# Norming the first chunk's mixer outputs in two steps, with the convolution's heads last

## What is computed

```python
def _mixer_block(h, w_in, ..., g_head_out, w_out):
    proj = h @ w_in                                   # 11 pieces of 256 columns
    out_a = _sgu_mixer(su, sv, w_sgu, b_sgu, g_sgu_v)
    out_b = _dilated_mixer(qd, kd, heads(dv)).reshape(B, S, MIX_W)
    out_c = _short_conv_mixer(cb, cc, cx, conv_w)
    out_d = _stick_breaking(qs, ks, heads(bv)).reshape(B, S, MIX_W)
    cat = jnp.concatenate([out_a, out_b, out_c, out_d], axis=-1).reshape(B, S, N_MIX_HEADS, HEAD_DIM)
    cat = _rms(cat, g_head_out.reshape(N_MIX_HEADS, HEAD_DIM)).reshape(B, S, D_MODEL)
    return cat @ w_out

def chunk(xc):                                        # retrieval, 128 tokens
    q = (xc @ w_q).reshape(C, PEER_HEADS, 2, PEER_HALF)
    ...                                               # top 16 pairs of keys per head: eidx, g
    a = jnp.einsum('thkd,td->thk', u_tab[eidx], xc)
    w = g * jax.nn.gelu(a)
    return jnp.einsum('thk,thkd->td', w, v_tab[eidx])
```

## Time and profile before

| what | value |
|---|---|
| time, median of 3 runs | 2979.73 us (2978.29 to 2980.22) |
| the profiled execution | 2974.2 us |
| its span, first to last instruction | 2972.4 us |
| TensorE busy | 2661.7 us (90%) |
| VectorE busy | 2007.6 us (68%) |
| ScalarE busy | 1501.0 us (50%) |
| moved by DMA | 1198.56 MB, mean 403 GB/s |

### The profile page before, as it was taken

One profiled execution on the slowest core, in us unless ns is written; L12 is line 12 of the kernel. 1 busy time (PEld: TensorE's weight loads), 2 busy tenths in 40 slices (PEclk: granted clock), 3 DMA queues, 4 the chain that ended last, 5 costly groups with the idle time before them and its releaser, 6 DMA issues.

```text
span 2972.4 us, 29543 instructions
## 1 busy us (share of the span) xinstructions
PE 2661.7 (90%) x8492; PEld 1468.9 (49%) x8492; DVE 2007.6 (68%) x5227; ACT 1501.0 (50%) x4099; POOL 1159.0 (39%) x1028
## 2 busy tenths in 40 slices
PE   8998989999999879998899988999989988777777
PEld 7753555754565335654455544654456533222222
DVE  3478678767689964556557987577668897454444
ACT  3246546468355543448434564458825554333333
POOL 0233433235434434344433444334434344343332
PEclk9999999999999989999999999999999999999999
DMA  5699999889999999999999999999999999999998
GB/s 231 245 398 421 415 421 421 359 358 407 421 421 421 421 411 419 421 421 408 421 421 405 421 421 421 420 406 421 421 421 411 380 422 421 422 421 422 422 421 347
DMA packets 167343, 1198.56 MB, mean 403 GB/s; under 512 B 19856, under 2 KB 20112, under 8 KB 22160
## 3 DMA queue, kind: packets, MB, share of 16 engines
q0 software_dynamic: 147456, 1073.81, 87.2%
q1 hardware_dynamic: 19728, 122.87, 10.2%
HBM read 1194.50 MB, written 2.10 MB: 403 GB/s over the span
## 4 chain that ended last, share of the span: by engine, by line
DMA 32%; PE 31%; DVE 7%; ACT 7%; issue 2%; POOL 0%; SPq 0%; POOLq 0%; ACTq 0%; DVEq 0%
DMA ring<-in_uv,idx 31%; PE psY L1271 21%; PE psP L1151 4%; DVE ring L1550 3%; PE psP L1144 3%; ACT L915 1%; ACT L1106 1%; ACT ring L1115 1%; ACT wgt L1111 1%; ACT gl L1106 1%; DMA wr<-in_w_out 0%; PE psO L1237 0%; POOL ring L892 0%; PE psT L1129 0%; DVE fm L1520 0%
## 5 line engine op out<-in xcount | busy, mean ns | idle before, releaser
L1271 PE MATMUL psY<-ring 128*128 128x512 f32 x3916 | 1840.7, 613 | 256.3 <-ACT ring L1115 251.7
L892 POOL DMA_INDIRECT ring<-in_uv,idx x1024 | 1158.8, 1132 | 1785.2 <-PE psY L1271 1545.5
L1550 DVE CUSTOM_DVE_ANT_0 ring<-ring,htok 128x1024 f32<-128x1024 f32 x1024 | 1239.4, 1222 | 673.0 <-DMA ring<-in_uv,idx 667.1
L1271 PEld LDWEIGHTS psY<-ring 128*128 128x128 f32 x3916 | 726.1, 194 | 1219.0 <-issue 1211.4
L1106 ACT ACTIVATE gl<-adot 128x1 f32<-128x1 f32 x1024 | 204.8, 200 | 1006.8 <-DVE adot L1550 1003.6
L1115 ACT ACTIVATE ring<-cst,wgt 128x128 f32<-128x128 f32 x979 | 393.2, 402 | 31.9
L1111 ACT ACTIVATE wgt<-gate,gl 128x1 f32<-128x1 f32 x1024 | 301.7, 295 | 33.2
L1144 PE MATMUL psP<-hT,wr 128*128 128x256 f32 (+1 forms) x1632 | 306.0, 345 | 0.0
L1144 PEld LDWEIGHTS psP<-hT,wr 128*128 128x128 f32 x1632 | 267.6, 192 | 42.1 <-issue 16.2
L1151 PE MATMUL psP<-wr,hT 128*128 128x256 f32 x1152 | 261.8, 383 | 7.3 <-issue 4.9
L1151 PEld LDWEIGHTS psP<-wr,hT 128*128 128x128 f32 x1152 | 220.7, 192 | 60.9 <-issue 27.3
(11 more groups left out here) (149 smaller groups left out, 1452.6 us busy)
## 6 DMA issues: line engine op xcount, KB each, us to landing
wr<-in_w_q SPq DMA_DIRECT2D x40, 1024.0 KB, 9.2
wr<-in_w_in SPq DMA_DIRECT2D x34, 1024.0 KB, 9.2
wr<-in_w_out SPq DMA_DIRECT2D x17, 1024.0 KB, 9.0
ring<-in_uv,idx POOLq DMA_INDIRECT x1024, 18.8
ring<-in_w_in SPq DMA_DIRECT2D x10, 1024.0 KB, 15.9
probs<-in_subkeys SPq DMA_DIRECT2D x5, 1024.0 KB, 16.9
ring<-in_w_out SPq DMA_DIRECT2D x3, 1024.0 KB, 5.0
cat<-in_g_ffn SPq DMA_DIRECT2D x5, 512.0 KB, 12.4
```

Of the source, the lines that this page charges most:

```text
L892: pool.indirect_dma_start(out=ring[:, q % NR], out_offset=None, in_=tables[s // NC], in_offset=bass.IndirectOffsetOnAxis(ap=idx[:, s % NS, ...
L1271: last = nc.tensor.matmul(psY[:, b * 512:(b + 1) * 512], ring[:, r % NR, 0:P], ring[:, r % NR, D + b * 512:D + (b + 1) * 512], start=first ...
L1550: v.tensor_tensor_reduce(out=u, in0=u, in1=htok[:, q // SLOTS % NS], scale=1.0, scalar=0.0, op0=ALU.mult, op1=ALU.add, accum_out=adot[:, J ...
```

## The change

For step 0 alone the norm over `cat` is made in two steps, and for all steps the mixers' places in `cat` change from A, B, C, D to A, B, D, C (`w_out` and the gains are permuted to match on the way in). `cat squares`, `cat` and `catT` of step 0 now cover A, B and D: 768 columns, 12 heads, six transposes. `stick out` of step 0 no longer waits for the convolution. Four new parts follow: `conv squares` (ScalarE, 256 columns), `cat conv` (VectorE: reduction, root and product on 4 heads), `catT conv` (two transposes on TensorE, two copies on ScalarE). The second half of an output piece of step 0 waits for `catT conv`. The planner may now open an output piece of step 0 while an input piece of step 1 is still open; halves are finished in the order in which pieces were begun, and no piece of another step is begun while one of step 0 is open. SyncE's load of the second norm's gains waits for `cat conv` in place of `cat`.

```diff
+        if s == 0:
+            p += [(out + 3.2, "act", "conv squares", s, 0), (out + 4.2, "dve", "cat conv", s, 0), (out + 5.2, "pe", "catT conv", s, 0),
+                  (out + 5.4, "act", "catT conv", s, 0)]
...
+    if s == 0 and (eng, part) in (("dve", "cat"), ("pe", "catT"), ("act", "catT"), ("act", "cat squares")):
+        return {"cat": 3.9, "catT": 0.8 if eng == "pe" else 1.8, "cat squares": 0.9}[part]
...
+        if s == 0 and N_IN <= i < first_q:
+            d += [("act", "catT conv", 0, 0)]
...
-            if eng == "pe" and class_of(key)[2] and soon():
+            if eng == "pe" and class_of(key)[2] and not any(s == 0 for s, _ in begun) and soon():
+                continue
+            if (eng, part) == ("pe", "rest of piece") and begun[0] != key[2:]:
+                continue
+            if (eng, part) == ("pe", "piece") and key[2] and 0 in [s for s, _ in begun]:
                 continue
...
-                sp.wait_ge(normed, NORMED_NO["cat", last] + 1)
+                sp.wait_ge(normed, NORMED_NO["cat" if last else "cat conv", last] + 1)
...
-                    take_batch(BATCH_NO["conv", s, 0], cat[:, 2], MW)
+                    take_batch(BATCH_NO["conv", s, 0], cat[:, 3], MW)
...
+                elif part == "conv squares":
+                    act.wait_ge(tp_taken, BATCH_NO["conv", s, 0] + 1)
+                    nc.scalar.activation(sq[:, 3 * MW:], cat[:, 3], ACT.Square).then_inc(cat_squared, 1)
...
+                    if s == 0 and N_IN <= i < N_IN + N_OUT:
+                        pe.wait_ge(tp_taken, BATCH_NO["catT conv", s, 0] + 1)
                     project(s, i, 1)
...
+                    heads = slice(0, 16) if s else slice(0, 12) if part == "cat" else slice(12, 16)
+                    m = heads.stop - heads.start
...
                 if part == "stick out":
-                    dve.wait_ge(tp_taken, BATCH_NO["conv", s, 0] + 1)
                     if s:
+                        dve.wait_ge(tp_taken, BATCH_NO["conv", s, 0] + 1)
```

More of the change, by code:

```diff
@@ L157, in cost @@
                     "v squares": 0.4, "dil exp": 0.3 + 0.1 * w, "dil taken": 0.2 + 0.1 * w, "logits": 1.2, "log part": 1.3, "stick exp": 0.7,
[L158 removed]
+                    "conv taken": 0.4, "cat squares": 1.1, "conv squares": 0.4, "catT conv": 0.7, "queries": 0.6, "key scores": 0.4, "gate exp": 0.6},
             "dve": {"norm1": 2.9, "qk": 5.0, "bias": 0.3 + 0.15 * w, "weigh": 0.2 + 0.15 * w, "dil out": 0.6, "softplus": 1.3,
[L160 removed]
+                    "exponent": 1.2, "stick out": 0.4, "sgu in": 3.2, "sgu": 0.7, "conv": 2.6, "cat": 4.6, "cat conv": 2.7, "out": 0.35 * n,
                     "norm2": 3.6, "top keys": 2.6, "top pairs": 2.2, "top index": 2.9, "gate": 0.2}}[eng][part]
@@ L271, in needs @@
     elif (eng, part) == ("dve", "stick out"):
-        d += [("pe", "stick out", s, 0), ("act", "conv taken", s, 0), ("dve", "sgu", s, 0), ("dve", "dil out", s, 0)]
+        d += [("pe", "stick out", s, 0), ("dve", "sgu", s, 0), ("dve", "dil out", s, 0)]
+        if s:
+            d += [("act", "conv taken", s, 0)]
     elif part == "cat squares":
@@ L276, in needs @@
         d += [("act", "cat squares", s, 0)]
+    elif part == "conv squares":
+        d += [("act", "cat squares", s, 0), ("act", "conv taken", s, 0)]
+    elif part == "cat conv":
+        d += [("dve", "cat", s, 0), ("act", "conv squares", s, 0)]
+    elif part == "catT conv":
+        d += [("dve", "cat conv", s, 0)] if eng == "pe" else [("pe", "catT conv", s, 0), ("act", "catT", s, 0)]
     elif part == "catT":
@@ L495, in begin @@
             classes[class_of(key)].pop(0)
+            if key[:2] == ("pe", "piece"):
+                begun.append(key[2:])
+            if key[:2] == ("pe", "rest of piece"):
+                begun.remove(key[2:])
             if key[:2] == ("pe", "piece") and not N_IN <= key[3] < N_IN + N_OUT:
@@ L532, in plan_orders @@
                     state["x"] += 1
-                elif key[:2] in FREED and not (key[2] == 0 and key[:2] in ((eng, "exponent"), (eng, "stick out"))):
+                elif key[:2] in FREED and not (key[2] == 0 and key[:2] in (("dve", "exponent"), ("dve", "stick out"), ("pe", "catT"))):
                     left[FREED[key[:2]]] += 1
@@ L569 @@
 PSS_LIST = list(numbers("pe", "scores", "logits", "key scores"))
-HN_LIST = [(part, s) for part, s, _ in numbers("dve", "norm1", "qk", "sgu in", "cat", "norm2")]
+HN_LIST = [(part, s) for part, s, _ in numbers("dve", "norm1", "qk", "sgu in", "cat", "cat conv", "norm2")]
 BATCH_NO, _batches = {}, 0
-for _part, _s, _i in numbers("pe", "hT1", "qk", "dil T", "conv", "catT", "hT2"):
+for _part, _s, _i in numbers("pe", "hT1", "qk", "dil T", "conv", "catT", "catT conv", "hT2"):
     BATCH_NO[_part, _s, _i] = _batches
-    _batches += 1 if _part in ("dil T", "conv") else 2
+    _batches += 1 if _part in ("dil T", "conv", "catT conv") else 2
 V_NO, _counts = {}, [0, 0]
@@ L806, in hn_free @@
                 return (sgu_in, s + 1) if adds else (sumsq, NORM_NO["sgu in", s] + 1)
+            if part == "cat conv":
+                return tp_ready, BATCH_NO["catT conv", s, 0] + 1
             return tp_ready, BATCH_NO[{"norm1": "hT1", "qk": "qk", "cat": "catT", "norm2": "hT2"}[part], s, 0] + 2
@@ L940, in take_hT @@
                     else:
-                        for k in range(4):
+                        for k in range(2 if b and part == "catT" and s == 0 else 4):
                             last = nc.scalar.activation(hT[:, 4 * b + k, o], psT[:, n % 2, k * P:(k + 1) * P], ACT.Copy,
@@ L1057, in front @@
                     wait_for(act, hn_free("cat", s))
-                    nc.scalar.activation(sq[:], cat[:].rearrange("p a b -> p (a b)"), ACT.Square).then_inc(cat_squared, 1)
+                    w = 4 * MW if s else 3 * MW
+                    nc.scalar.activation(sq[:, :w], cat[:].rearrange("p a b -> p (a b)")[:, :w], ACT.Square).then_inc(cat_squared, 1)
+                elif part == "conv squares":
+                    act.wait_ge(tp_taken, BATCH_NO["conv", s, 0] + 1)
+                    nc.scalar.activation(sq[:, 3 * MW:], cat[:, 3], ACT.Square).then_inc(cat_squared, 1)
+                elif part == "catT conv":
+                    n = BATCH_NO["catT conv", s, 0]
+                    act.wait_ge(tp_ready, n + 1)
+                    for k in range(2):
+                        last = nc.scalar.activation(hT[:, 6 + k, 0:P], psT[:, n % 2, k * P:(k + 1) * P], ACT.Copy,
+                                                    scale=gain_t[:, 1, 6 + k:7 + k])
+                    last.then_inc(tp_taken, 1)
                 elif part == "catT":
@@ L1194, in front @@
                     for b in range(2):
-                        transposes(BATCH_NO[part, s, 0] + b, [t[:, (4 * b + k) * P:(4 * b + k + 1) * P] for k in range(4)])
+                        transposes(BATCH_NO[part, s, 0] + b, [t[:, (4 * b + k) * P:(4 * b + k + 1) * P]
+                                                              for k in range(2 if b and part == "catT" and s == 0 else 4)])
+                elif part == "catT conv":
+                    pe.wait_ge(normed, NORMED_NO["cat conv", s] + 1)
+                    transposes(BATCH_NO["catT conv", s, 0], [hn[:, k * P:(k + 1) * P] for k in (6, 7)])
                 elif part == "piece":
```

47 lines of the change are left out of this document (25 added, 22 removed).

## The result

The changed kernel takes 2985.49 us (median of 15 runs) beside 2978.43 us for the kernel before (15 runs, on the same chip): a ratio of 1.0023, with a 95% interval of 1.0015 to 1.0031. It is 7.1 us slower, where 12.5 were forecast; 2992.2 us was the number, in a range from 2978 to 3000. The profiled executions stand further apart, 2984.5 us (span 2982.7) against 2974.2 (2972.4): 10.3 us.

What follows compares the result with a forecast made beforehand. The kernel was taken as bound by its DMA engines, other work costing only where it idles them. Terms 0.6 + 1.2 - 1.5 + 12.2 = 12.5 us, added to the median, gave 2992.2 us, range 2978 to 3000.

Steps and rivals of the forecast that it cites:

- The front: Step 0 up to the first gather: two-step norm and moved half piece send it out at 114.4, +0.6 us.
- The second head: Step 0's second head, 166 to 171 us: one more dot product stands ahead of its `top index`, +1.2 us.
- The pieces: Input pieces of steps 2 and 3: stall at 583 to 608 us spread out, hardly shortened, -1.5 us (-15 to +5).
- TensorE was simply behind: Pieces of steps 2 and 3: TensorE's total work makes the stall, so rows between pieces gain little of a possible 17 us.
- The seam: Between steps 3 and 4: `top keys` waits for step 3's addition, no gather can be queued, engines run dry, +12.2 us.
- The rest moves without a price: Everywhere else: leads of `top index` over its gather change by a few rows, no cost seen.
- The base: Median of the kernel before, to which the sum was added; its profiled execution, 2974.2 us, lay 5.5 us below.
- (1): Steps 2 and 3: evenly spread rows remove most of the stall (-15); -1.0 us in all, 2979 us, chance 0.12.
- (3): Stall at 583 to 608 goes, first gather 1.1 us earlier, seam costs only 8; -8 us, 2971.6 us, chance 0.07.
- (2): Between steps 3 and 4: seam covered by loads or given back, costing +3; 3.3 us in all, 2983 us, chance 0.10.
- (4): Stall of steps 2 and 3 grows by 5, seam costs 16; 22.8 us in all, 3002.5 us, chance 0.09.
- (5): Whole kernel: the change does not do what it says, first gather at 113.8, nothing else differs; chance 0.02.

Runs made afterwards that it cites:

- four_moves: before_dil_out_later plus three moves: step 0's second-head numbers before dot 12, head (4, 0)'s before dot 506, `v` 778 before dot 780; 2970.72 us, ratio 0.9982.
- six_moves: four_moves, with `v` rows 144 and 148 also put between the three pieces of steps 2 and 3; 2970.76 us, ratio 0.9979.
- rows_between: The kernel before, with `v` rows 144 and 148 put between the three pieces of steps 2 and 3 on TensorE; 2976.67 us, ratio 1.0002.
- before_dil_out_later: The kernel before, with the output of mixer B's first head of step 2 moved on TensorE behind the first of three pieces; 2970.98 us, ratio 0.9981.
- after_pieces_together: The changed kernel, with the last three input pieces of steps 2 and 3 together again ahead of row 134; 2991.35 us, ratio 1.0050.
- order_only: The changed kernel's order everywhere else, but step 0's norm in one step as in the kernel before; 2985.99 us, ratio 1.0032.
- before_seam_late: The kernel before, with step 3's closing addition, then the first heads' keys, pairs and index of steps 4 and 5, behind dot 511; 2995.44 us, ratio 1.0065.

## Why the prediction was right and wrong

**The front (+0.6): right, a little less.** The first half was forecast for 76.5 (76.59), the last of the four additions for 92.4 (92.33), the first gather for 114.4 (114.41). With the start of the copy taken out it is +0.31: the half begins 8.92 us behind the copy where I had 9.1. The root did not shrink with its width, 2.2 us on 4 heads (73.65 to 75.83) as on 12 (70.07 to 72.33). That start-up varies by 1.5 us I had not seen, and the agreement of 114.4 is partly luck.

**The second head (+1.2): right.** Its gather follows the first by 55.03 us, before by 53.96; over all profiles it is 55.0 to 55.8 in the changed order and 53.8 to 54.0 in that of before, 1.1 to 2.1 more. (Its numbers moved ahead of dot 12 as well gave 52.96 in four_moves and 54.01 in six_moves, which settles nothing.) Start-up (0.3), front (0.3) and this (1.1) are most of the +2.3 of the curve.

**The pieces (-1.5): mis-sized, measured -6.4. This is the step that failed.** For the new order the sum had eleven pieces, 15 `v` and two transposes, 104.5 us, "and with as much waiting 109.5". In the profile after:

```profile
482.99 1.43 POOL L921 DMA_INDIRECT ring<-in_uv,idx  x1 [0.78 <-PE psY L1317]
...
583.44 3.62 PE L1184 MATMUL psP<-hT,wr 128*128 128x256 f32 x16
```

From the gather that `v` 116 sets free to the end of piece 10 at 587.06 it is 104.1 us. The work was summed rightly; the 5 us of waiting were not there (TensorE waits 0.64 us in all that time). With the 5.4 us less the term would have been -6.9. Most of the waiting belonged to one place of the old order, and the rows that I had quoted held its mark: the three pieces took 23.07 us, 7.69 each and not 6.9, at a clock of 0.93 over that stretch. I carried the wait over as if every order had it, and so missed that the new order escapes both a wait of 3.77 us and the low clock behind it. The mechanism, "TensorE was simply behind", held in the order of before: rows spread among the pieces gained nothing there (rows_between), and TensorE's time decided (before_dil_out_later). In the new order it was not all: with the pieces together and at full clock the time is 5.2 to 8 us longer (after_pieces_together). The term came out far on the good side of the forecast's value, within its ends (-15 to +5). (The 111.5 us of its idle sum should be 111.7, which changes nothing.)

**The seam (+12.2): right in kind, under-sized; measured +15.5.** The chain from the last dot's start to the gather's issue was given as 13.5 and is 13.28. Four smaller terms missed. The rows do not stop landing at once: from 1585 to 1591 the engines' GB/s fall to 266, 94, 25, which is 4.2 us idle that the sum lacked, and from 1591 to the start of the last dot it is another 0.5. The way from issue to data was taken as 2.2 us; here the engines move 426 GB/s from 1606.0, 1.2 us behind the issue. And of the weight load, taken as 1.0, only 0.6 us fell into the gap: nothing moves from 1591 to 1604 (1 GB/s), and the load starts just ahead of the gather (82 GB/s from 1604.0 to 1604.8).

```profile
1606.00:1607.00 1.00, 1.00 (x6) 0.87 (x6) 1.00 (x7) 0.42 (x3) 0.94 (x1) 1.00 1.00 426
```

With +4.2 for the ragged end, +0.5 up to the dot, -1.0 for the way, +0.4 for the load, -0.2 for the chain and -0.4 for the 2.9 us (not 2.5) idle before, 12.2 becomes 15.7, beside 15.5 from the curve. Since the load was under way, the seam does not show the way by itself. The 2.2 us I had misread: the earlier trace rows gives the first gather's stretch a share of 0.03, and 0.03 of 16 us is half a microsecond of work at its end. In a narrow stretch of the kernel before it stands there:

```profile
115.00:116.00 1.00, 1.00 (x12) 1.00 (x11) 0.00 (x0) 0.95 (x4) 0.79 (x1) 1.00 0.48 115
```

A share of 0.48 in that microsecond is all sixteen engines from about 115.5 on. So data came some 1.7 us behind the issue there (1.6 in the profile after, 114.41 to 116.0). The Trainium skill's figure (DMA: Bandwidth & Descriptors, "Specifications"), about 1 us of first-byte latency on GpSimd's path, was the nearer one for the seam, where full rate came 1.2 us behind the issue, and is short of the 1.6 to 1.7 us of the first gathers.

**"The rest moves without a price": wrong by some -3.** Behind the seam 4.4 came back (4.3 in order_only). before_seam_late gives back 3.0 with the old order, so most of it goes with a long stall and should have been a term of the seam. Whether the later front of steps 4 and 5 cost anything stays open: the curve has +1.2 there for the changed kernel and -2.6 for order_only, which has the same order.

**The base.** By the profiles the change costs 10.3 us against a forecast of 12.5. The medians say 7.1, since the profiled execution of before was a quick one. Of the 5.4 us that the forecast of the change is too high, 2.2 are terms of the sum and 3.2 lie between profile and median. That the sum came within 2.2 us is partly luck: by the curve it was 4.9 too high at the pieces and some 3 behind the seam, and 3.3 too low in the seam, and about 2 us more came at the very end (8.4 by bytes, 10.3 by the last dot). The number itself, 2992.2, is 6.7 above 2985.49; the other 1.3 are the base, 2979.73 over 3 runs and 2978.43 over 15.

The rivals: (1) and (3), the stall mostly gone, did not happen, though the pieces came nearly half way to them (-6.4 for -15); (2), a covered seam, is ruled out by before_seam_late; (4) had the seam's size (16), but the stall shrank where it was to grow; (5) is ruled out by the orders.

## What to carry to other kernels

A planner that is played through anew moves parts far from the edit; here the edit itself cost 0.3 us and one head's place, 1500 us later, cost 15 us, so compare the two orders wherever a producer of addresses stands near the end of a stream. Before summing an engine's work in a stretch, take its durations from that stretch: the block that took 23.07 us here, where 21 are usual, had a wait ahead of it, and moving that wait under the block was the best single edit of this study (2970.98 us, ratio 0.9981 to before). And before spreading or gathering a block, ask who is fed meanwhile: the same three pieces together cost 5.2 to 8 us in one order, and two rows put between them gained nothing in the other. A gain in the mean of the DMA engines is worth only what the slowest of them gains (7.3 us by bytes and 3.4 by the last dot in four_moves).

## What was not expected of the hardware

One DMA engine's share of the work is finished behind all the others': shares of 0.06 for 8 us at the end of four_moves, and for about 2 us in the seam (1589 to 1591) and at 585 to 587 in the kernel before. Which engine it is, and what it carries besides, the trace does not say. That later stalls get shorter behind a long one (3.0 us in before_seam_late, by the curve) would fit an engine that catches up in it; this was not tested.

TensorE's clock fell to 0.50 with a wait of 3.77 us (1.2 GHz) and was back at 1.00 (2.4 GHz) from 587. In after the like happens with a wait of 3.17 us: 0.50 from 598 to nearly 604. In before_dil_out_later, without such a wait, it stays at 1.00 through the pieces.
